# Softmax of six attentions: the maximum taken off inside ScalarE's exponential, head by head, with the sums from the same instruction

## The reference, cut to what matters

```python
s = jnp.einsum('bqhd,bkhd->bhqk', q, k) * scale    # plus a bias or mask
p = jax.nn.softmax(s, axis=-1)                           # exp(s - max) / sum exp(s - max)
return jnp.einsum('bhqk,bkhd->bqhd', p.astype(v.dtype), v)
```

## Time and profile before

| | us |
|---|---|
| median of 3 runs | 3082.63 |
| lowest and highest | 3080.7, 3084.58 |
| profiled execution, its own time | 3073.08 |
| its span in the trace | 3071.2 |
| TensorE matmuls busy (share of the span) | 2844.9 (93%) |
| VectorE busy | 1287.3 (42%) |
| ScalarE busy | 1232.4 (40%) |
| GpSimd busy | 2059.3 (67%) |

### The profile page before, as it was taken

One profiled execution on the slowest core, in us unless ns is written; L12 is line 12 of the kernel. 1 busy time (PEld: TensorE's weight loads), 2 busy tenths in 40 slices (PEclk: granted clock), 3 DMA queues, 4 the chain that ended last, 5 costly groups with the idle time before them and its releaser, 6 DMA issues.

```text
span 3071.2 us, 46378 instructions
## 1 busy us (share of the span) xinstructions
PE 2844.9 (93%) x18990; PEld 2598.2 (85%) x18990; DVE 1287.3 (42%) x1553; ACT 1232.4 (40%) x1538; POOL 2059.3 (67%) x896
## 2 busy tenths in 40 slices
PE   7999879999988987999999999889999999988998
PEld 6898678799877877879989899877998989988798
DVE  2651374623424137453243423756424232375523
ACT  4344424444424442444444433324444443333443
POOL 7777445788856644578888774337888877425786
PEclk9999989999999998999999999989999999999999
DMA  6455323555575542355555554125555555423554
GB/s 214 159 198 192 130 83 107 169 189 179 199 168 178 189 143 76 105 197 185 186 188 185 166 177 145 63 82 185 187 179 194 186 167 175 138 69 103 181 189 145
DMA packets 132106, 487.77 MB, mean 159 GB/s; under 512 B 14608, under 2 KB 14608, under 8 KB 130896
## 3 DMA queue, kind: packets, MB, share of 16 engines
q1 hardware_dynamic: 127296, 463.53, 45.1%
q0 software_dynamic: 4624, 21.48, 2.7%
HBM read 478.65 MB, written 6.29 MB: 158 GB/s over the span
## 4 chain that ended last, share of the span: by engine, by line
PE 77%; DVE 12%; DMA 3%; issue 3%; ACT 3%; POOL 1%; DVEq 0%; SPq 0%; POOLq 0%
PE psA L343 47%; PE psY L343 28%; DMA ring<-in_weights 3%; PE psT L394 2%; DVE Sc L1226 1%; DVE st L1221 1%; DVE arena L1300 1%; POOL rest L969 1%; ACT Sc L1697 1%; DVE xT_upper L1304 1%; DVE Sc L1216 1%; DVE x L1172 1%; DVE xT_rest L1305 1%; ACT upper L1697 1%; DVE Sc L1481 0%
## 5 line engine op out<-in xcount | busy, mean ns | idle before, releaser
L969 POOL TENSOR_TENSOR rest<-ring,upper 128x1024 fp32r<-128x1024 f32 (+1 forms) x832 | 2020.8, 2444 | 885.5 <-ACT upper L1697 876.8
L1697 ACT ACTIVATE upper<-ring 128x1024 fp32r<-128x1024 f32 (+1 forms) x832 | 867.9, 1051 | 967.5 <-DMA ring<-in_weights 966.5
L343 PE MATMUL psA<-xT_upper,upper 128*128 128x256 f32 x2944 | 412.7, 283 | 12.2 <-ACT upper L1697 9.2
L343 PE MATMUL psA<-xT_rest,upper 128*128 128x256 f32 x2944 | 413.9, 283 | 0.0
L343 PEld LDWEIGHTS psA<-xT_upper,upper 128*128 128x128 f32 x2944 | 385.7, 189 | 26.9 <-issue 9.9
L343 PE MATMUL psA<-xT_upper,rest 128*128 128x256 f32 x2944 | 406.4, 280 | 0.3 <-POOL rest L969 0.3
L1198 DVE TENSOR_TENSOR sil<-sil,psA 128x256 f32<-128x256 f32 x144 | 60.7, 421 | 802.6 <-ACT sil L1697 802.6
L343 PEld LDWEIGHTS psA<-xT_rest,upper 128*128 128x128 f32 x2944 | 380.5, 192 | 0.0
L343 PEld LDWEIGHTS psA<-xT_upper,rest 128*128 128x128 f32 x2944 | 373.6, 189 | 0.5 <-POOL rest L969 0.5
L343 PE MATMUL psY<-upper,hT_upper 128*128 128x512 f32 x704 | 206.9, 399 | 23.2 <-DVE hT_rest L1201 19.2
L343 PE MATMUL psY<-upper,hT_rest 128*128 128x512 f32 x704 | 208.0, 401 | 0.0
(11 more groups left out here) (234 smaller groups left out, 3530.1 us busy)
## 6 DMA issues: line engine op xcount, KB each, us to landing
ring<-in_weights SPq DMA_DIRECT2D x880, 512.0 KB, 3.4
G<-in_rows POOLq DMA_DIRECT2D x6, 1024.0 KB, 7.4
rel_by_distance<-G POOLq DMA_DIRECT2D x1, 4096.0 KB, 45.8
G<-in_rows POOLq DMA_DIRECT2D x7, 512.0 KB, 6.0
arena<-rel_by_distance POOLq DMA_DIRECT2D x1, 2048.0 KB, 14.2
x<-in_x SPq DMA_DIRECT2D x2, 512.0 KB, 5.6
par<-in_params POOLq DMA_DIRECT2D x4, 256.0 KB, 6.1
xn<-in_mem POOLq DMA_DIRECT2D x1, 1024.0 KB, 9.5
```

The lines of the kernel that those rows point to most:

```text
L343: i = pe.matmul(out, lhsT, rhs, start=start, stop=stop)
L969: pool.tensor_tensor(rest[:, r, 0:n], ring[:, r, 0:n], upper[:, r, 0:n], ALU.subtract)\
L1697: act.activation(out, in_, func, **kw).then_inc(*up)
```

## The change

VectorE takes the negated maximum and hands it over at once; ScalarE runs one exponential per head, with the negated maximum of that head as the bias and the sum of the head's exponentials as a second output. VectorE's subtraction over the scores and its sum are gone. With a sink, the negated maximum is the lesser of itself and the negated sink, `below`, which is filled once per layer; the sink's own term is now an addition. The sums get two sets of columns that alternate, and the reciprocal a place of its own. `weigh` takes the tile before it (`last`) and first waits for its own read of that tile's outputs. In ScalarE's queue the wait for the sink's exponential (`linked`) goes.

```diff
@@ soften, VectorE
                 m = st[:, 32 + 4 * (n % 2):36 + 4 * (n % 2)]
-                link(dve.tensor_reduce(m, sc, AX, ALU.max))
-                if sink is not None:
-                    link(tt_(m, m, sink[:, 4 * hb:4 * hb + 4], ALU.max))
+                if sink is None:
+                    dve.tensor_reduce(m, sc, AX, ALU.max, negate=True).then_inc(*sig["shift"].up((name, hb, qt)))
+                else:
+                    link(dve.tensor_reduce(m, sc, AX, ALU.max, negate=True))
+                    tt_(m, m, below[:, 4 * hb:4 * hb + 4], ALU.min).then_inc(*sig["shift"].up((name, hb, qt)))
                     sk = st[:, 40 + 4 * (n % 2):44 + 4 * (n % 2)]
-                    tt_(sk, sink[:, 4 * hb:4 * hb + 4], m, ALU.subtract).then_inc(*sig["sink shifted"].up((name, hb, qt)))
-                tt_(sc, sc, m.unsqueeze(2).broadcast_to([P, 4, w]), ALU.subtract)\
-                    .then_inc(*sig["shifted"].up((name, hb, qt)))
-
-            def weigh(name, n, hb, qt, w, dv, sink, gate, first):
-
+                    dve.wait_ge(*sig["shift"].after((name, hb, qt)))
+                    tt_(sk, sink[:, 4 * hb:4 * hb + 4], m, ALU.add).then_inc(*sig["sink shifted"].up((name, hb, qt)))
+
+            def weigh(name, n, hb, qt, w, dv, sink, gate, first, last):
+
+                if last is not None:
+                    dve.wait_ge(*taken(("o", name) + last))
                 dve.wait_ge(*sig["weights"].after((name, hb, qt)))
-                sums, r = st[:, 48:52], st[:, 52:56]
-                link(dve.tensor_reduce(sums, Sc[:, n % 2, :, 0:w], AX, ALU.add))
+                sums, r = st[:, 48 + 4 * (n % 2):52 + 4 * (n % 2)], st[:, 121:125]
@@ block2, VectorE
                 scale_x()
+                ts_(below, par[:, 441:449], -1.0, None, ALU.mult).then_inc(*sig["vector step"].up())
@@ attention, ScalarE
                         go(sk, sk, ACT.Exp, step())
-                    act.wait_ge(*sig["shifted"].after((name, hb, qt)))
-                    sc = Sc[:, n % 2, :, 0:kts * P]
-                    if sink:
-                        linked()
-                    go(sc, sc, ACT.Exp, sig["weights"].up((name, hb, qt)))
+                    act.wait_ge(*sig["shift"].after((name, hb, qt)))
+                    for j in range(4):
+                        sc = Sc[:, n % 2, j, 0:kts * P]
+                        m, total = (st[:, c + 4 * (n % 2) + j:c + 4 * (n % 2) + j + 1] for c in (32, 48))
+                        go(sc, sc, ACT.Exp, sig["weights"].up((name, hb, qt)) if j == 3 else step(), bias=m, accum_out=total)
```

More of the change, by code:

```diff
@@ L1263, in attention @@
                     if n:
-                        weigh(name, n - 1, *todo[n - 1], width(todo[n - 1][1]), dv, sink, gate, first)
+                        weigh(name, n - 1, *todo[n - 1], width(todo[n - 1][1]), dv, sink, gate, first,
+                              todo[n - 2] if n > 1 else None)
                 n = len(todo)
-                weigh(name, n - 1, *todo[n - 1], width(todo[n - 1][1]), dv, sink, gate, first)
+                weigh(name, n - 1, *todo[n - 1], width(todo[n - 1][1]), dv, sink, gate, first, todo[n - 2])
             def turned(name, br, gain=None):
@@ L1305, in merge @@
                                 tt_(xT[1][:, v, :], o, xT[0][:, v, :], ALU.subtract).then_inc(*sig["merged parts"].up(n))
+            below = st[:, 128:136]
             causal_bias = lambda hb, b, c, w: CM[:, c:c + w].unsqueeze(1).broadcast_to([P, 2, w])
```

## The result

| | before | changed | ratio (95%) |
|---|---|---|---|
| median, us (runs) | 3081.66 (4) | 3043.80 (4) | 0.9877 (0.984 to 0.9914) |
| lowest and highest, us | 3079.89, 3084.58 | 3033.47, 3055.29 | |

Its profiled execution is the slowest of the four: 3055.29 us, with a span of 3053.5. Against the profiled execution of before (3073.08) that is 17.8 us.

The account below looks back on a forecast made before the run. TensorE matmuls are 75% of the chain, so softmax matters only where TensorE waits for it. Per layer -7.1 us (second block) and -2.3 (first), twice each, make -18.8 from 3082.63: about 3064, range 3049 to 3076.

Parts of the forecast that it names:

- slc tile 3: Second-block attention, large tile: TensorE's 2.56 us wait for its exponential would go, -2.56 us per layer.
- swa tile 0: Second-block attention: the 4.0 us wait for OT_rest, behind a narrow and a wide subtraction, shrinks by 1.5 us per layer.
- swa tile 3: Second-block attention: 2.65 us wait, held by the 4-element sink operation beside GpSimd, stays; 0 us.
- fox tile 0: Second-block attention: the 3.2 us wait for OT_rest shrinks by 1.2 us per layer, one wide subtraction being in front.
- fox tile 3: Second-block attention, wide tile: its 2.16 us wait shrinks by 0.35 us per layer.
- mem tile 0: First-block attention: the OT_rest wait of 5.1 us, behind two wide subtractions, shrinks by 2.3 us per layer.
- behind slc tile 3: Transposes and gate piece after that wait, 5.33 us at mean clock 0.68, gain 1.6 us per layer from the clock.
- The heads' length: ScalarE's four exponentials per tile: 0.47 us a wide head, 1.97 us a wide tile, +0.9 over the single exponential.
- rival 1: Clock stays full behind fox tile 0 and fox tile 3: some 1.2 and 3.3 us more per layer, 3055; chance 0.17.
- Some 5 for the merges: Part of the forecast's own bounds, in us, for merges whose lengths differ by 4.9 us without any change.
- rival 2: Merges give the gain back through VectorE additions stalled beside GpSimd: two more stops +16, 3080; chance of most back 0.08.
- Rivals 3 and 4: 3: heads do not overlap, about 3102, chance 0.04. 4: the change doesn't do what it says, 3073, chance 0.08.

Follow-up runs that it names:

- Experiment 5: Changed kernel with the sink's exponential moved behind the four heads in ScalarE's queue: 3043.69 us, ratio 0.9903 to the kernel before.
- experiment 2: Changed kernel with the sums put back on VectorE, so the bias alone: 3045.48 us, ratio 0.9913 to the kernel before.
- experiment 3: Kernel before with four exponentials that give the sums, without bias; VectorE's subtraction stays, its sum goes: 3080.55 us, ratio 1.0024.
- experiment 8: Kernel before with 28, 22 and 36 unused matmuls in the three OT_rest waits (swa, fox, mem tile 0): 3058.64 us, ratio 0.9961.
- experiment 4: Kernel before with its exponential cut into four heads, nothing else: 3064.36 us, ratio 0.9978.
- experiment 9: Changed kernel with sums on VectorE, sink's exponential behind the heads, and 16, 14 and 18 unused matmuls in the OT_rest waits: 3024.57 us, ratio 0.984 to before.

## Why the prediction was right or wrong

The figures are differences in us between the first profiles of the two kernels, one for each of the two layers of that block. Waits are from matmul to matmul, so a little longer than the idle time in brackets. "Between" is the same work between the waits.

| | predicted | measured, by layer |
|---|---|---|
| slc tile 3, wait | -2.56 | -2.46, -2.48 |
| win tile 0 | +0.2 | +0.29, +0.29 |
| swa tile 0, OT_rest | -1.5 | -1.64, -1.64 |
| swa tile 3 | 0 | -0.02, -0.02 |
| fox tile 0, OT_rest | -1.2 | -1.26, -1.26 |
| fox tile 3 | -0.35 | -0.24, -0.24 |
| mem tile 0, OT_rest | -2.3 | -2.23, -2.23 |
| behind slc tile 3 | -1.6 | -1.55, -1.51 |
| behind swa tile 0 | none | -1.25, -1.42 |
| behind fox tile 0 | none | -1.25, -1.51 |
| behind swa tile 3 | none | -1.39, +0.20 |
| behind fox tile 3 | none | -0.73, 0.00 |

**The waits: right, place by place.** The seven of the table, over the layers, came to -15.1 us, against -15.4 forecast (slc tile 0 and win tile 3, +0.2 and -0.3 us, can't be told from the work around them). That VectorE was late by its own subtraction at slc tile 3, that OT_rest stands behind one or two subtractions in VectorE's queue, and that swa tile 3 is held by the sink's 4 elements, is what the rows show. Experiment 5 shows the last, experiments 2 and 3 that the subtraction alone, and not the sum, was in OT_rest's way. At slc tile 3 the reason was narrower than the forecast had it: the disturbed length of the subtraction (2.78 us), not the subtraction as such. Where it took 0.69 us (experiment 8), the wait was 0.60 us with all of VectorE's softmax in place.

**The heads' length: right,** 0.49 us from start to start against 0.47 taken, 2.06 us a wide tile against 1.97. The Trainium skill ("ScalarE: Activation LUTs", rules for kernel authors) budgets 0.3 us and 0.83 ns an element for an activation with a pointer bias, an estimate of 0.51 us for a head without a read. One such instruction lasts 0.497 us here, but the next one starts 0.40 us after it (experiment 2), so four in a row cost less than the rule has it. Two slips in the forecast's working changed nothing in its sum: 3 x 0.47 + 0.37 + 0.2 is 1.98, and the lower bound of 0.36 a head gives +0.6 us a tile, not +0.5.

**The clock: the step that failed.** The term "the clock behind slc tile 3" was right to 0.1 us and then used at one place per layer. The same price fell due behind swa tile 0, which the forecast did not look at for it, and behind fox tile 0, which it left to rival 1 at a chance of 0.17. Between those waits the attentions became 10.9 us shorter (1.0, 0.7, 6.1 and 3.2 by layer), where 3.4 were forecast. In the trace's clock rows, TensorE is at its lower level for 83.0 us of the four stretches before and for 52.6 after. Rival 1 was right for fox tile 0 and wrong for fox tile 3, whose clock only went from 0.50 to 0.57. With the term at the three places that came out in both layers, the forecast would have been -18.8 - 2 x 2.7 = -24.2, of the -26.1 measured. Even so the price isn't fixed: behind swa tile 0 and fox tile 0 of the first second-block layer the second profile of before took 8.42 and 8.37 us in place of 7.01 and 7.02, with the waits as they were, and the third of the changed kernel 7.27 in place of 5.76 behind swa tile 0.

**The range: the second step that failed.** "Some 5 for the merges" was drawn from two merges of one trace. The three runs of before lay within 4 us of each other, and I read that as the spread of a run. Later the kernel before spread over 29 us in 25 runs, with a standard deviation of 8.1 us about a mean of 3072.4; the changed kernel's sixteen later runs have means of 3053.4 and 3052.6. Against these, the first median of before is 9 us high and that of the changed kernel 9 us low, and that is nearly all of what separates -37.9 from -20. The forecast carried the difference to a base that was itself a draw.

**What stays open.** The attentions give 26 us in each profile, and two of three timed comparisons give less, 20 and 14.5. All stages outside them, from the first matmul on, sum to 2645.2 and 2646.0 us in the two traces of before and to 2653.7, 2644.3 and 2641.5 in the three of the changed kernel. In the last two, which fell among their kernel's faster runs, nothing is given back; in the first, which is the slowest of its four, 8 us are. The run times say more than such single traces. Over all 73 later runs of before the mean is 3071.9 us, over the 16 later ones of the changed kernel 3053.0: -18.9, with a standard error of 2.1 if the runs are taken as independent. If the attentions of the runs without a profile are those of the profiles, some 7 us come back outside them on average. The same reckoning gives +6.0 us outside for experiment 8, +5.4 for experiment 3, -4.8 for experiment 4 and -6.4 for experiment 9 (standard errors of 2 to 3), though no step touches those stages. What does it wasn't tried. That -18.9 is the forecast's -18.8 is luck: the attentions gave 7 us more than forecast, and about as much was lost where the forecast had no term. Nor can I say whether the first comparison differs by chance or by its chip.

**The other rivals.** What rival 2 describes is real, but it is a lottery in stages with back-to-back rests, feed-forward as well as merge, in both kernels. The long addition of the earlier trace rows itself stands in none of the three traces of the changed kernel, nor in the second of before; the second block's merges took 82.0 to 87.1 us in the changed kernel's three traces, inside the 80 to 88 forecast. Rivals 3 and 4 are out: the heads overlap, and all places did what they should. No wait appeared before the tiles 1 and 2.

## What to carry to other kernels

Price a wait of TensorE as the wait plus the slower work behind it, at every wait that gets shorter and not only where it vanishes: here mostly 1.3 to 1.5 us each, beside the 1.3 to 2.5 that the waits themselves gave. Of a change with two halves, time each alone: here taking the maximum off by a bias brought everything, and giving the sums out of the exponential cost 0.1 us a head. To judge a change of a few tenths of a per cent, compare the stages it touches, cut by the same matmuls in both traces, and take the run-to-run spread from many runs, not from three that happen to agree.

## What the runs showed that I had not expected

- The same wait doesn't always have the same price, not even in the same kernel. Behind 2.63 us the granted clock over the next 50 matmuls was 1.00 in two profiles of the changed kernel and 0.77 in the third, and behind 4.27 us it was 0.80 in one profile of before and 0.65 in the other. What decides it, these runs don't show.
- 13 to 36 unused matmuls in a wait keep the clock at 1.00 behind it, and take 1.25 to 2.7 us off the work that follows, without making the wait itself longer (the fillers read data long in place, and end before what TensorE waits for).
- A 128x256 cast on VectorE, 0.29 us by itself, took 16.33 us beside back-to-back operations of GpSimd. GpSimd's rests take 2.4 us each, so some seven of them passed while the cast stood. The longest such cast, in the third profile of the changed kernel, took 20.6 us.
- Which engine began first went with the length of VectorE's 128x512 subtraction at slc tile 2, in all ten places of the five traces that have it: 2.61 to 2.86 us where GpSimd's rest had begun 0.06 to 0.31 us earlier, 0.69 where the rest came 0.10 to 0.76 us later. Some 3.7 us of TensorE's time per layer hang on it.
- Taking VectorE's operation of 1.2 us per tile out of its queue (experiment 3) changed no wait for OT_rest at all: both stayed at 7.2 us together.
